# Router on the raw residual, its weights stationary in four column groups, in a hybrid decoder layer with 32 experts

## The chip, the cores and the metric

The kernel runs on one core of a Trainium2 chip. The metric is device time in microseconds (us) of one execution; the number for the kernel before is the median of three runs. A profile is one further execution, taken by the hardware profiler; its own span stands beside the median below.

## The reference

One layer over 256 tokens of width 1024: a mixer (gated linear attention and dilated window attention), a cross-attention into 256 memory tokens, a mixture of experts, and a final RMSNorm. What matters here is the third part:

```python
f = rms_norm(h, norm3_g)                       # h * rsqrt(mean(h^2) + eps) * g
logits = f @ w_router + b_router               # 256 x 32
top_logit, top_e = lax.top_k(logits, 4)
gate = jax.nn.softmax(top_logit, axis=-1)
# every token goes to its 4 experts e, weighted by gate:
glu = x @ w_gate[e] + b_gate[e]
lin = x @ w_up[e] + b_up[e]
y = clamped_swiglu(glu, lin) @ w_down[e] + b_down[e]
h = h + sum(gate * y)
out = rms_norm(h, final_norm_g)
```

All of it is in 32-bit floats. The 32 experts have three 1024 x 1024 matrices each: 12 MB an expert, 384 MB in all.

## The kernel before, in words

Five engines run their own instruction lists and meet at semaphores. Tokens lie in two tiles (t = 0, 1) of 128 partitions; `h` (128 x 2 x 1024) is the residual. PSUM has eight banks, and a table written out by hand (`FILLS`) gives each product its bank in turn; `take(name)` waits until the bank of that name is filled, `emptied(name)` until it has been read, `fill(name)` until it may be written again.

**Weights of the experts.** The ring in SBUF holds 16 slots of 1 MB. SyncE issues the loads in order, one 1 MB unit each, twelve units an expert (`load`, L381: four pairs of w_gate and w_up, then four of w_down). The first units are issued while the mixer and the cross-attention still run, as slots come free; sixteen are all the ring holds. Unit 16 and later wait in `slot_left` for TensorE to finish with the slot (L388): `gu_used` after a quarter of an expert's gate and up products, `dn_used` after a quarter of the down product.

**From the cross-attention to the first expert.** The output projection makes four banks `xo{n}{t}` (half n of the width, tile t; L1291). VectorE adds each to `h` (L1121), ScalarE squares the sum (`squares`, L556). TensorE then puts `h` into the four accumulator banks by products with the identity (L1539). `normed(3, ...)` sums the squares (L869), asks for the root (L822), GpSimd raises to -1/2 (`root`, L454), VectorE scales `h` into `f` (L872), TensorE transposes `f` (L1303), ScalarE and VectorE multiply by the norm's gain into `fT` (L760, L1128). The router follows: a product with ones for the bias (L1545), then for each of eight chunks of the width and each tile the 128 x 128 chunk of `fT` as weights and 32 columns of `w_rt` as the moving side (L1550). VectorE copies the logits (L1135), takes the largest eight and their places (L1138, L1141), makes the one-hot mask (L1146, L1148), then the gates (L1150 to L1153). TensorE counts places with a triangular matrix (L1556 to L1560) and transposes the gates (L1564), which ScalarE copies into `gateT`. Meanwhile ScalarE and VectorE cut `f` into two f16 parts in the memory of `h` (`f16`; L518, L1132).

**The experts** run as a loop over eight groups of four, the function `body(n, k)` on every engine. VectorE builds the selection matrices `sel` (L1178) and the gated ones `selG` (L1185). TensorE gathers the tokens of the group in four products (`gather`, L1584) through banks 2 and 3, of which `gather(2)` and `gather(3)` come after the first quarter of the first expert; ScalarE and VectorE multiply by the gain into `xg` (L781, L1192). Per expert j: gate and up products (L1624, two 64-column groups side by side), copies `hs` by ScalarE and VectorE (L518, L1197), transposes (L1638), the activation (L1208 to L1218), the down product (L1652) and the scatter into the accumulators (L1594).

## Time and profile before

| what | us |
|---|---|
| median of three runs (lowest, highest) | 1304.59 (1302.69, 1306.29) |
| span of the profiled execution | 1304.8 |
| TensorE busy | 1166.9 (89%) |
| VectorE busy | 413.0 (32%) |
| ScalarE busy | 279.5 (21%) |
| q1, the queue of the weight loads: bytes, share of 16 engines' span | 455.11 MB, 86.9% |

The profiled execution is 0.2 us above the median and inside the spread of the runs. In the page's chain of work that ended last TensorE has 57% and DMA 30%. The page also cuts the span in 40 slices of 32.6 us, each with a digit for the busy share of an engine and with what the DMA engines moved. Busy shares are averages over stages with different limits, so the stages have to be read one at a time.

### The profile page before, as it was taken

The page shows a single profiled execution, that of the slowest core. Times are in us where ns is not written, and L with a number is a line of the kernel's source. Part 1 is how long each engine was busy: PE and PEld are TensorE (multiplying, and loading weights), DVE is VectorE, ACT ScalarE, POOL GpSimd, SP SyncE. Part 2 cuts the span into 40 slices and gives each one's busy share as a digit, 9 for nine tenths or more (in the row PEclk, how much of TensorE's full clock was granted, in tenths as well). Part 3 has the DMA queues.
Part 4 walks back from the last instruction along what each step waited for, and adds up shares of the span by engine and source line. Part 5 has one row for each costly group of instructions (what it writes and reads, how often), then busy time and mean ns, then how long its engine had stood idle before and what let it go on. Part 6 is the DMA issues. An engine that isn't in the chain of part 4 may idle for free.

```text
span 1304.8 us, 16913 instructions
## 1 busy us (share of the span) xinstructions
PE 1166.9 (89%) x6669; PEld 596.7 (46%) x6669; DVE 413.0 (32%) x816; ACT 279.5 (21%) x475; POOL 20.2 (2%) x43
## 2 busy tenths in 40 slices
PE   6999999999899999898889988988988899889886
PEld 5888988987533333333323323322333233233322
DVE  5688454566411321121222112111212221121112
ACT  5655454455310020011002001100110020011001
POOL 3000000000000000000000000000000000000000
PEclk9999999999899999999999999999999999999997
DMA  8666443696299999999999999999999999999992
GB/s 277 194 194 191 146 128 105 220 366 266 85 371 423 421 422 421 422 422 422 422 422 422 422 422 421 422 422 422 422 423 421 422 422 422 422 422 422 422 422 105
DMA packets 103983, 458.00 MB, mean 351 GB/s; under 512 B 7324, under 2 KB 50392, under 8 KB 54792
## 3 DMA queue, kind: packets, MB, share of 16 engines
q1 hardware_dynamic: 103008, 455.11, 86.9%
q0 software_dynamic: 848, 2.32, 0.6%
q8 instruction: 28, 0.46, 0.1%
q14 instruction: 11, 0.09, 0.0%
q10 hardware_dynamic: 88, 0.02, 0.0%
HBM read 456.37 MB, written 1.05 MB: 351 GB/s over the span
## 4 chain that ended last, share of the span: by engine, by line
PE 57%; DMA 30%; DVE 6%; SPq 3%; issue 2%; ACT 2%; DVEq 0%; POOL 0%; POOLq 0%; ACTq 0%
DMA ring<-in_w_up 29%; PE bank L1624 19%; PE bank L1652 10%; PE bank L1268 7%; PE bank L1291 5%; PE bank L1341 5%; SPq L381 3%; PE bank L1584 2%; PE bank L1403 1%; DVE ring L843 1%; PE bank L1594 1%; PE bank L1638 1%; ACT ring L541 1%; DMA ring<-in_w_in 1%; DVE reg_g L1214 1%
## 5 line engine op out<-in xcount | busy, mean ns | idle before, releaser
L1624 PE MATMUL bank<-ring,reg_a 128*64 128x512 f32 x2048 | 457.9, 595 | 62.1 <-DMA ring<-in_w_up 60.1
L1624 PEld LDWEIGHTS bank<-ring,reg_a 128*64 128x64 f32 x2048 | 152.5, 137 | 355.3 <-issue 352.8
L1652 PE MATMUL bank<-ring,reg_g 128*64 128x512 f32 x1024 | 237.0, 617 | 20.9 <-DVE reg_g L1218 20.9
L1197 DVE COPY reg_t<-bank 128x512 f32<-128x512 f32 x32 | 22.1, 691 | 610.7 <-PE bank L1624 610.7
L518 ACT ACTIVATE reg_t<-bank 128x512 f32<-128x512 f32 x64 | 38.2, 597 | 678.3 <-PE bank L1624 473.7
L1652 PEld LDWEIGHTS bank<-ring,reg_g 128*64 128x64 f32 x1024 | 73.0, 141 | 178.5 <-issue 135.8
L843 DVE SCALAR_TENSOR_TENSOR ring<-ring 128x2048 f16<-128x2048 f32 x36 | 82.2, 2289 | 46.7 <-ACT ring L541 46.6
L541 ACT ACTIVATE ring<-ring 128x2048 f16<-128x2048 f32 x36 | 68.3, 1908 | 17.2 <-PE bank L1341 6.8
L1594 PE MATMUL bank<-reg_t,reg_g 64*128 64x512 f32 x256 | 63.6, 615 | 5.6 <-ACT reg_t L518 5.6
L1268 PE MATMUL bank<-reg_a,ring 128*128 128x256 f16 x576 | 65.4, 276 | 2.8 <-DVE reg_a L851 2.8
L1341 PE MATMUL bank<-reg_a,ring 128*128 128x256 f16 x576 | 63.2, 273 | 0.0
L1268 PEld LDWEIGHTS bank<-reg_a,ring 128*128 128x128 f16 x576 | 56.6, 99 | 11.7 <-DVE ring L843 3.2
L1341 PEld LDWEIGHTS bank<-reg_a,ring 128*128 128x128 f16 x576 | 56.3, 98 | 6.8 <-issue 0.3
L1291 PE MATMUL bank<-ring,reg_a 128*128 128x256 f16 x480 | 53.4, 273 | 0.0
L1638 PE MATMUL bank<-ident,reg_t 128*128 128x128 f32 x256 | 34.1, 276 | 21.1 <-DVE reg_t L1197 21.1
L1291 PEld LDWEIGHTS bank<-ring,reg_a 128*128 128x128 f16 x480 | 46.6, 98 | 5.9 <-issue 0.2
L792 ACT ACTIVATE reg_g<-reg_g 128x256 f32<-128x256 f32 x64 | 26.7, 417 | 100.8 <-DVE reg_g L1209 100.7
L1638 PEld LDWEIGHTS bank<-ident,reg_t 128*128 128x128 f32 x256 | 27.4, 140 | 42.0 <-ACT reg_t L518 41.5
L1192 DVE TENSOR_TENSOR reg_a<-bank,g 128x512 f32<-128x512 f32 x16 | 11.1, 692 | 91.7 <-PE bank L1584 91.7
L1594 PEld LDWEIGHTS bank<-reg_t,reg_g 64*128 64x128 f32 x256 | 22.0, 186 | 31.7 <-issue 19.1
L1208 DVE TENSOR_TENSOR reg_g<-bank,bT 128x256 f32<-128x256 f32 x64 | 26.8, 419 | 22.0 <-PE bank L1638 22.0
L1584 PE MATMUL bank<-reg_t,h 128*128 128x256 f16 x256 | 32.2, 282 | 0.9 <-ACT reg_o L518 0.9
(248 smaller groups left out, 811.7 us busy)
## 6 DMA issues: line engine op xcount, KB each, us to landing
ring<-in_w_gate SPq DMA_DIRECT2D x128, 1024.0 KB, 26.5
ring<-in_w_up SPq DMA_DIRECT2D x128, 1024.0 KB, 26.9
ring<-in_w_down SPq DMA_DIRECT2D x128, 1024.0 KB, 26.9
ring<-in_w_in SPq DMA_DIRECT2D x24, 1024.0 KB, 5.6
ring<-in_w_branch_gate SPq DMA_DIRECT2D x8, 1024.0 KB, 5.2
ring<-in_w_xkv SPq DMA_DIRECT2D x4, 1024.0 KB, 4.9
ring<-in_w_mix_out SPq DMA_DIRECT2D x4, 1024.0 KB, 5.2
ring<-in_w_branch_gla SPq DMA_DIRECT2D x2, 1024.0 KB, 4.9
```

The costliest lines, as they stand in the source:

```text
L381: sp.dma_start(slot[s], src.rearrange("e p n -> p (e n)")).then_inc(late_ld[s], 16)
L518: return act.activation(dst, src, ACT.Copy)
L541: ins = act.activation(cut[u % EARLY][:, 0, :], raw[u % EARLY], ACT.Copy, scale=WS)
L843: ins = dve.scalar_tensor_tensor(cut[u % EARLY][:, 1, :], raw[u % EARLY], WS, cut[u % EARLY][:, 0, :], ALU.mult, ALU.subtract)
L1268: ins = mm(b[:, i * T:(i + 1) * T], w[:, pw, c, o:o + P], rhs[:, px, c, :], start=(c == 0 and k == 0), stop=(c == nk - 1 and k == 2))
L1291: ins = mm(b[:, i * n:(i + 1) * n], lhs[:, px, c, t * P:(t + 1) * P], w[:, pw, c, 0:n], start=(c == 0 and k == 0), stop=(c == nk - 1 and k ...
L1341: ins = mm(b[:, i * T:(i + 1) * T], w[:, pw, i, c, :], aT[:, px, c, :], start=(c == 0 and k == 0), stop=(c == C - 1 and k == 2))
L1584: ins = mm(pt[2 + q % 2][:, i * T:(i + 1) * T], f16[:, part, t, 2 * q + i, :], sel[:, t, :], start=(t == 0 and part == 0), stop=(t == TT - ...
L1594: mm(acc[t][nh][:], selT[rows_h, j, t, :], y[rows_h, :], start=False, stop=False)
L1624: ins = mm(pt[nh][col:col + 64, :], xe[c], w[:, i, nh * 512:(nh + 1) * 512], start=(c == 0), stop=(c == C - 1))
L1638: ins = pe.transpose(pt[i][:, c * P:(c + 1) * P], hs[:, 4 * i + c, :], ident[:])
L1652: ins = mm(pt[2][64 * nh:64 * nh + 64, :], actT[:, c, :], w[:, i, nh * 512:(nh + 1) * 512], start=(c == 0), stop=(c == C - 1))
```

## The change

- The router works on `h` before the norm's scale. TensorE transposes `h` itself (`residual_T`): the first quarter ahead of the last output bank `xo11`, the others behind it. ScalarE and VectorE multiply by the gain (`routed_T`) as before; the first quarter is multiplied ahead of ScalarE's last squares, the second ahead of VectorE's sum of squares, the fourth while GpSimd makes the root.
- The router's product has `w_rt` (128 x 32) as weights and `fT` (256 columns) as the moving side; chunk c goes to the 32 output partitions of column group c mod 4. VectorE copies the result (`rtp`), and a product with `fold` (four stacked 32 x 32 identities, made once at the start) adds the groups and turns the logits token by token. The norm's scale and the bias, now broadcast to all partitions, are applied to the logits.
- The f16 parts are cut from `h` with the norm's scale and lie in the region of the former `f`. VectorE cuts the low parts in two halves (`f_lows`): one after the mask, one in the first group.
- The accumulator's products with the identity move: tile 0's behind the router, tile 1's behind the counts.
- The first group of experts is peeled off the loop. The low parts' second half, the reciprocal and the gates are computed there by VectorE behind `sel`; the gates' transposes run between the first two experts, and ScalarE copies `gateT` there.
- Channels are in chunks of 128 in place of strides of 8: w_gate, w_up, w_down, w_router and norm3_g are laid out anew on the host, the biases' transposes read contiguously, and the copies `hs` are contiguous. TensorE waits for ScalarE's half of `hs` before its first four transposes and for VectorE's before the other four.

```diff
-FILLS += [f"f_T{i}" for i in range(4)] + ["rt", "pos", "all", "gT"]
+FILLS += [f"f_T{i}" for i in range(4)] + ["rt", "rl", "pos", "all"]
@@ expert_groups
-            with eng.Fori(0, GROUPS) as n:
-                body(n, n)
+            body(0, 0, True)
+            with eng.Fori(1, GROUPS) as n:
+                body(n, n, False)
@@ scalar
+            def routed_T(q):
                 b = take(act, f"f_T{q}")
                 for i in range(2):
                     c = 2 * q + i
                     ins = act.activation(fT[:, c, :], b[:, i * T:(i + 1) * T], ACT.Copy, scale=g3[:, c:c + 1])
                 ins.then_inc(free_bank(f"f_T{q}"), 1)
+            for n in range(2):
+                for t in range(TT):
+                    emptied(act, f"xo{n}{t}")
+                    squares(3, h, xn, t, n, 512)
+                    if (n, t) == (1, 0):
+                        routed_T(0)
+            routed_T(2)
+            act.wait_ge(root_done, 6)
             for t in range(TT):
-                copy(f16[:, 0, t], f[:, t]).then_inc(f_high, 1)
+                act.activation(f16[:, 0, t], h[:, t, :].rearrange("p (c n) -> p c n", c=C), ACT.Copy,
+                               scale=st[:, 6 + t:7 + t]).then_inc(f_high, 1)
@@ vector
-            normed(3, 2, lambda t: h[:, t, :].rearrange("p (q c) -> p c q", c=C), lambda t: f[:, t], 6)
+            routed_T(1)
+            squared[0] += TT * 2
+            dve.wait_ge(norm_ss, squared[0])
+            link(dve.reduce_sum(st[:, 6:8], ssq[:, 3, :, 0:2], AX))
+            dve.tensor_scalar(st[:, 6:8], st[:, 6:8], 1.0 / D, EPS, ALU.mult, ALU.add).then_inc(root_asked, 1)
+            roots[0] += 1
+            routed_T(3)
+            b = take(dve, "rt")
+            dve.tensor_copy(rtp, b[:, 0:T]).then_inc(free_bank("rt"), 1)
+            dve.wait_ge(root_done, roots[0])
+            b = take(dve, "rl")
             for t in range(TT):
+                ins = dve.scalar_tensor_tensor(logit[:, t, :], b[:, t * E:(t + 1) * E], st[:, 6 + t:7 + t], b_rt[:],
+                                               ALU.mult, ALU.add)
...
             dve.reduce_sum(mask, hot.rearrange("p (t k) e -> p t e k", t=TT), AX).then_inc(gate_ready, 1)
-            dve.wait_ge(top_exp, 2)
-            link(dve.reciprocal(st[:, 54:56], st[:, 54:56]))
...
+            f_lows(0)
             b = take(dve, "pos")
...
+            def gates_and_lows():
+                f_lows(1)
+                dve.wait_ge(top_exp, 2)
+                link(dve.reciprocal(st[:, 54:56], st[:, 54:56]))
...
@@ vector, body, behind sel
+                if first:
+                    gates_and_lows()
+                    dve.wait_ge(gate_ready, 2)
@@ tensor
             for n in range(2):
                 w = weights(f"xo{n}")
                 for t in range(TT):
+                    if (n, t) == (1, 1):
+                        residual_T(0)
                     token_major(f"xo{n}{t}", w, oxT, 4, (t,), 512, ...)
+            for q in range(1, 4):
+                residual_T(q)
+            pe.wait_ge(ld_route, 48)
+            b = fill("rt")
+            for c in range(C):
+                if c % 2 == 0:
+                    emptied(pe, f"f_T{c // 2}")
+                j = c % 4
+                ins = mm(b[32 * j:32 * j + 32, 0:T], w_rt[:, c, :], fT[:, c, :], start=(c < 4), stop=(c >= 4))
+            filled(ins, "rt")
+            emptied(pe, "rt")
+            b = fill("rl")
+            for t in range(TT):
+                ins = mm(b[:, t * E:(t + 1) * E], rtp[:, t * P:(t + 1) * P], fold[:], start=True, stop=True)
+            filled(ins, "rl")
...
+            residual(0)
             pe.wait_ge(gate_ready, 1)
...
+            residual(1)
@@ tensor, body
                     if q >= 2:
                         pe.wait_ge((xg_act, xg_dve)[q - 2], 2 * k + 1)
+                        if first:
+                            pe.wait_ge(f_low, 2 * TT)
...
+                    if first and j == 1:
+                        gates_T()
...
-                    pe.wait_ge(hs_act, k * EG + (j + 1))
-                    pe.wait_ge(hs_dve, k * EG + (j + 1))
                     for i in range(2):
+                        pe.wait_ge((hs_act, hs_dve)[i], k * EG + (j + 1))
                         for c in range(4):
                             ins = pe.transpose(pt[i][:, c * P:(c + 1) * P], hs[:, 4 * i + c, :], ident[:])
@@ kernel (host)
+    for name in ("w_gate", "w_up", "w_down"):
+        w = np.asarray(inputs[name])[0]
+        inputs[name] = w.reshape(E, C, P, D).transpose(0, 2, 1, 3).reshape(E, P, C * D)
```

## Rows read from the trace of the kernel before

**Rows 1.** The page's slices: what the DMA engines moved, 40 slices of 32.6 us.

```profile
GB/s 277 194 194 191 146 128 105 220 366 266 85 371 423 421 422 421 422 422 422 422 422 422 422 422 421 422 422 422 422 423 421 422 422 422 422 422 422 422 422 105
```

**Rows 2.** Stages: busy us (instructions) of PE, PEld, DVE, ACT, POOL; PEclk; DMA share; GB/s.

```profile
340.00:360.00 20.00, 16.14 (x93) 11.40 (x94) 11.17 (x29) 6.90 (x15) 0.00 (x0) 0.74 0.09 32
360.00:365.00 5.00, 5.00 (x33) 2.62 (x34) 0.69 (x1) 0.84 (x2) 0.00 (x0) 1.00 0.81 297
...
1100.00:1200.00 100.00, 86.74 (x410) 32.32 (x410) 21.48 (x53) 11.32 (x20) 0.00 (x0) 0.98 1.01 422
```

**Rows 3.** The chain that ended last, near its end: start, us, what.

```profile
1244.61 26.92 DMA ring<-in_w_up
...
1271.66 3.67 PE bank L1624 x16
```

**Rows 4.** SyncE's queue in order of time: start, us, the loads it issued.

```profile
335.97 0.33 SPq L381 DMA_DIRECT2D ring<-in_w_up  x1
360.04 0.33 SPq L381 DMA_DIRECT2D ring<-in_w_gate  x1
...
365.48 0.33 SPq L381 DMA_DIRECT2D ring<-in_w_gate  x1
```

**Rows 5.** The chain that ended last, 335.9 to 362 us: start, us, what.

```profile
335.98 0.70 DVE h L1121
...
337.90 0.72 POOL st L454
...
338.65 2.21 DVE reg_m L872 x2
...
340.91 1.75 PE bank L1303 x14
...
343.02 4.34 PE bank L1550 x32
...
347.63 0.30 DVE reg_l L1138 x2
...
349.15 0.60 DVE route L1148
...
352.55 0.43 issue
352.99 3.43 PE bank L1584 x16
356.42 3.58 PE bank L1624 x16
```

**Rows 6.** Groups by line and form: busy us, mean ns of one | idle before.

```profile
L1128 DVE TENSOR_TENSOR reg_a<-bank,g 128x512 f32<-128x512 f32 x2 | 1.4, 692 | 1.1 <-PE bank L1303 1.0
L1132 DVE TENSOR_TENSOR h<-reg_m,h 128x1024 f16<-128x1024 f32 x2 | 2.4, 1222 | 0.7 <-ACT h L518 0.7
L1185 DVE TENSOR_TENSOR reg_g<-reg_t,route 128x512 f32<-128x512 f16 x2 | 1.3, 686 | 0.1
L1135 DVE COPY reg_l<-bank 128x64 f32<-128x64 f32 x1 | 0.2, 223 | 0.9 <-PE bank L1550 0.9
```

**Rows 7.** TensorE in order of time: start, us, operation, count, idle before it.

```profile
311.48 3.62 PE L1493 MATMUL bank<-reg_l 128*128 128x256 f32 x16
...
335.78 3.60 PE L1539 MATMUL bank<-h,ident 128*128 128x512 f32 x8
...
359.94 1.92 PE L1584 MATMUL bank<-reg_t,h 128*128 128x256 f16 x16
...
361.79 10.52 PE L1624 MATMUL bank<-ring,reg_a 128*64 128x512 f32 x48
```

**Rows 8.** VectorE in order of time, columns as in Rows 7.

```profile
350.50 0.58 DVE L1153 TENSOR_REDUCE route<-reg_g 128x64 f32<-128x256 f32 x1
...
351.69 0.76 DVE L1178 TENSOR_TENSOR reg_t<-route,iota_s 128x256 f16<-128x256 f32 x2
```

**Rows 9.** Granted clock of TensorE (PEclk) in one stretch; columns as in Rows 2.

```profile
346.00:356.00 10.00, 6.69 (x32) 5.21 (x32) 6.31 (x24) 3.36 (x9) 0.00 (x0) 0.50 0.00 0
```

More of the change, by code:

```diff
@@ L208, in _program @@
         hs = region(reg_t, 0, C, P)
+        rtp = region(reg_t, 0, T)
         y = region(reg_t, 1024, 512)
@@ L750, in _ @@
             x_out_T(1)
-            for n in range(2):
-                for t in range(TT):
-                    emptied(act, f"xo{n}{t}")
-                    squares(3, h, xn, t, n, 512)
             act.wait_ge(ld_route, 48)
-            for q in (0, 2):
+            def routed_T(q):
                 b = take(act, f"f_T{q}")
@@ L771, in _, with body @@
             copy(totals, b[:, 0:E]).then_inc(free_bank("all"), 1)
-            b = take(act, "gT")
-            copy(gateT[0:E, :], b[0:E, 0:T]).then_inc(free_bank("gT"), 1)
-            def body(n, k):
+            def body(n, k, first):
                 for q in (0, 2):
@@ L1122, in _, with routed_T @@
                         .then_inc(free_bank(f"xo{n}{t}"), 1)
-            normed(3, 2, lambda t: h[:, t, :].rearrange("p (q c) -> p c q", c=C), lambda t: f[:, t], 6)
             dve.wait_ge(ld_route, 48)
-            for q in (1, 3):
+            def routed_T(q):
                 b = take(dve, f"f_T{q}")
@@ L1527, in _, with residual_T @@
             x_out(1)
+            def residual_T(q):
+                b = fill(f"f_T{q}")
+                for t in range(TT):
+                    emptied(pe, f"xo{q // 2}{t}")
+                    for i in range(2):
+                        c = 2 * q + i
+                        ins = pe.transpose(b[:, i * T + t * P:i * T + (t + 1) * P], h[:, t, c * P:(c + 1) * P], ident[:])
+                filled(ins, f"f_T{q}")
             for n in range(2):
@@ L1535, in _, with residual @@
                 pe.wait_ge(free[b], USES[b])
-            for n in range(2):
-                for t in range(TT):
-                    emptied(pe, f"xo{n}{t}")
+            def residual(t):
+                for n in range(2):
                     mm(acc[t][n][:], ident[:], h[:, t, n * 512:(n + 1) * 512], start=True, stop=False)
-            norm_transposes("f_T", lambda t, c: f[:, t, c, :], 8)
-            pe.wait_ge(ld_route, 48)
-            b = fill("rt")
-            mm(b[:, 0:TT * E], ones[0:1, :], mid(b_rt[:], TT), start=True, stop=False)
-            for c in range(C):
-                if c % 2 == 0:
-                    emptied(pe, f"f_T{c // 2}")
-                for t in range(TT):
-                    ins = mm(b[:, t * E:(t + 1) * E], fT[:, c, t * P:(t + 1) * P], w_rt[:, c, :], start=False,
-                             stop=(c == C - 1 and t == TT - 1))
-            filled(ins, "rt")
+            residual(0)
             pe.wait_ge(gate_ready, 1)
@@ L1560, in _, with gates_T @@
             filled(mm(b[:, 0:E], ones[:], mask[:, 1, :], start=False, stop=True), "all")
-            pe.wait_ge(gate_ready, 2)
-            b = fill("gT")
-            for t in range(TT):
-                ins = pe.transpose(b[0:E, t * P:(t + 1) * P], gate[:, t, :], ident[:])
-            filled(ins, "gT")
+            residual(1)
+            def gates_T():
+                pe.wait_ge(gate_ready, 2)
+                for t in range(TT):
+                    ins = pe.transpose(pt[3][0:E, t * P:(t + 1) * P], gate[:, t, :], ident[:])
+                ins.then_inc(gT_full, 1)
             for b in range(4):
@@ L1572, in _, with body @@
             per = 12 * EG
-            def body(n, k):
+            def body(n, k, first):
                 pe.wait_ge(sel_ready, k + 1)
@@ L1614, in body @@
                     v = 12 * j
+                    if first and j == 1:
+                        gates_T()
                     xe = [xg[:, c, j * SLOTS:(j + 1) * SLOTS] for c in range(C)]
@@ L1657, in body @@
                 scatter(EG - 1)
+                if first:
+                    pe.wait_ge(gT_done, 1)
             expert_groups(pe, body)
```

51 lines of the change are left out of this document (31 added, 20 removed).

## The prediction

> **What bounds the kernel now.** I read the slices first. From slice 12 to slice 38 (counted from 0) the DMA engines move 421 to 423 GB/s without a break, and just before, in slice 10, 85 GB/s [rows 1]. So 27 of 40 slices stream expert weights at one constant rate. A stage closer up gives the same: 422 GB/s at a DMA share of 1.01 from 1100 to 1200 us, while TensorE is busy 86.74 of the 100 us [rows 2]. The chain at the end says so too: the last gate and up product starts at 1271.66 us when a load of w_up has just landed, and only 33 us of work follow it [rows 3]. The expert stage is bound by bytes.
>
> The second thing to see is the hole before it. From 340 to 360 us the DMA share is 0.09 [rows 2]: all sixteen slots are full. SyncE issues unit 15 at 335.97 and the next one only at 360.04 [rows 4], when TensorE has finished the first quarter of the first expert. After that instant 368 units of 1 MB (1.049 million bytes) remain, at 422 GB/s 2.485 us each, 914 us. Nothing later in the stage makes up for a late start, and nothing takes back an early one. **The end follows the instant at which that first slot is released**, one us for one us. The work on the change is thus the chain from the last add into `h` (335.98) to the end of the first gate and up quarter (356.42 + 3.58 = 360.00), 24.0 us [rows 5].
>
> **The change along that chain.** I walk it with durations of before; the new clock time stands behind each step.
>
> 1. `residual_T(0)` goes ahead of the last output bank: four transposes. Fourteen took 1.75 us [rows 5], so four cost 0.5. The add starts at 336.45. This is the one new cost at the head.
> 2. Add, squares, sum and root request take as before 335.98 to 337.90: GpSimd's root starts at 338.4 and ends at 339.1. The other twelve transposes hide here, but for the half of them that wait for the add (337.2); the last ends at 338.1. GpSimd issues its two late loads (b_down, the final gain) half a us later too, and is still free by then.
> 3. Removed: the scaling of `h` into `f`, 2.21 us, the transposes behind it, 1.75, the bias product and the router's 32 short products, 4.34 [rows 5]. In their place: `routed_T(3)` on VectorE behind the root request, 0.69 [rows 6], to 339.1. ScalarE's `routed_T(2)` ends at 338.9, so the fourth quarter is the last. Then the last two of eight router products. One product of 256 columns is two instructions of 3.62/16 = 0.226 us [rows 7]. Two products side by side in their column groups are 0.45, one after the other 0.9. That groups of 64 columns run side by side is in the trace: 16 instructions of 512 columns in 3.58 us [rows 5], 0.22 each, against 3.60/8 = 0.45 for one over all columns [rows 7]. I take 0.45 and 0.1 for the semaphores: filled at 339.7 to 339.9. The first six are done by then.
> 4. Added: the copy `rtp` of 128 x 256. 128 x 64 took 0.22 and 128 x 512 took 0.69 [rows 6]; between them, 0.42. To 340.25. Then the fold, four instructions with full weights; L1550's went at 4.34/32 = 0.136 each [rows 5], so 0.6 with its start. Then two scalings of 128 x 32, at most 0.22 each [rows 6]: the first of the top-8 instructions starts at 341.35, against 347.63 [rows 5]. **6.3 us gained so far.**
> 5. From there to the mask is unchanged, 347.63 to 349.75 or 2.1 us [rows 5]: 343.5.
> 6. VectorE then has `f_lows(0)`, two instructions of 512 elements. An f16 low part of 1024 took 1.22 [rows 6]; half of it is 0.61, two are 1.25, to 344.75. Removed from this place: the gates' arithmetic, from 349.75 to 351.08, 1.3. Even. Placing and `sel` take what they took, 351.08 to 352.45 or 1.4 [rows 8]: ready at 346.15. The count products are hidden beside `f_lows(0)`.
> 7. TensorE's own queue: counts from 343.55, eight instructions at 0.136, to 344.6; then `residual(1)`, four instructions of 512 columns at 0.45 [rows 7], 1.8 us, to 346.4. So TensorE and VectorE arrive within 0.2 us of each other. `residual(0)` (341.0 to 342.8) hides beside the top-8. All eight of these instructions were hidden beside the norm before; if the clock is low they are not.
> 8. Removed: the gates' transposes, the copy to `gateT` and the 0.43 of issue between it and the first gather at 352.99 [rows 5]. Added in the first group: 0.3 us of transposes at the second expert. There TensorE is ahead of the loads, so this costs nothing; without that slack it would cost 0.3.
> 9. First gathers: 3.43 us [rows 5], at a granted clock of 0.50, that is 1.2 GHz [rows 9]. The same sixteen took 1.92 at the full 2.4 GHz [rows 7]. Starting at 346.45 with the full clock, they end at 348.4; the gain's multiply for the first quarter ends by about 348.5. The quarter of gate and up, 3.6 us, ends at **352.15 against 360.00: 7.85 us.**
>
> **What could hold the next slots.** The second pair of loads went out 5.4 us after the first [rows 4]. For that pair `gather(2)` waits for all low parts and `gather(3)` for VectorE's `xg`. Behind `sel` VectorE has `f_lows(1)` 1.25, gates 1.4 [rows 8], `selG` 1.35 [rows 6], `xg` 0.7: from 346.15 to 350.9, while TensorE asks at 352.15. 1.2 us of slack; queued behind these are only the activations of the first expert, ten us later. The DMA stage after the release is therefore a copy of the old one, shifted. Contiguous `hs` copies cost the same (one PSUM read per element), and the split wait gives at most 0.1 at the tail. The weights' new layout keeps 8 KB a partition at the same strides, so 422 GB/s stays. `fold` (0.2 us) and a broadcast bias are at the start, where VectorE waits for `x`: nothing.
>
> One rule to weigh. Step 3 leans on column groups, and the rows show two groups at twice the pace. The Trainium skill (TensorEngine Tiling (Array Packing), Theoretical Speedup and Key Properties) grants up to four times for 32 columns, but says that changing the tiling mode drains the engine. By the first half the eight products would be 0.9 us instead of 1.8, without effect, since the last pair waits for `routed_T(3)`; by the second, two changes would cost a drain each. No run yet shows four groups; at a change from the whole array to 64 columns the trace shows no gap: the gathers end at 361.86 and L1624 starts at 361.79 [rows 7].
>
> **Rivals.**
> - *The clock stays low.* Before, it was at 0.50 from 346 to 356 [rows 9], and what ran ahead of the fall was 4.34 us of 32-column products. After, TensorE from 338 to 345 has about 0.9 to 1.8 us of router, 1.8 of identity products, the fold and the counts, with holes between. If it falls there, the counts go from 1.1 to 1.9, `residual(1)` from 1.8 to 3.6, the gathers from 1.95 to 3.43: 4.1 us at most, leaving 3.75, or 1300.8. A fall for part of it costs 1.5 to 3: 5.6 left, about 1299. For it: nearly the same holes. Against it: dense 512- and 256-column products in place of the 32 short ones.
> - *Column groups one after the other.* The last pair costs 0.45 more and the six before it, 2.7 us from 338.1, end at 340.8: in all 1.8 late. 6.0 gained, 1298.5. The rows with two groups speak against it.
> - *The gain is not kept.* If the loads were starved after the early restart (from 360 to 365 us they moved 297 GB/s, not 422 [rows 2]) because slots are released late in the first group, the gain would go there: 1302 to 1304. Against: the steps between releases are the same as before.
> - *Slower.* VectorE's queue in the first group: `gather(2)` and `gather(3)` stand behind 4.8 us of new order, with 1.2 of slack. Each us beyond is paid in full; slower than before by over 0.3% needs 12.9 us beyond the plan there, say from the strided one-hot arithmetic of the gates taking ten times its 1.2 us. It would give 1309. The rows of exactly these instructions speak against it.
>
> **How the numbers follow.** The profiled span, 1304.8, is 0.2 above the median 1304.6. Likeliest is the full chain: 7.85, less 0.3 for some ten new semaphore handoffs at 0.03, so 7.5: 1304.6 - 7.5 = **1297.1**. Chances: 0.52 for this, 0.28 for the low clock, 0.08 for the groups in a row, 0.09 for no lasting gain, 0.03 for slower. The range takes in the first three and the spread of the runs (1.9 below to 1.7 above the median): 1295.2 to 1301.2. What can be told from no change is 0.3%, 3.9 us: faster 0.86, same 0.11, slower 0.03.
>
> **What the profile after would show.** First load behind the hole issued at about 352.5 instead of 360.04; top-8 at 341.4; `sel` ready at 346.15; PEclk above 0.9 from 340 to 356 if the likeliest case holds, two sixteens of L1584 of nearly 1.95 us each; 422 GB/s after. Wrong would be: a gather that waits for VectorE in the first group, eight router products taking over 2 us, DMA below 415 GB/s between 400 and 1200 us, or an end that moves less than the first load does.

## The result, and the profile after

The changed kernel takes 1294.45 us (median of 4 runs, 1292.22 to 1295.37) against 1304.32 for the kernel before in the same series (4 runs, 1302.69 to 1306.29): ratio 0.9923, 95% interval 0.991 to 0.9936. That is 9.9 us gained where 7.5 were forecast, and 0.75 us below the low end of the range. A second series, with 17 runs of the kernel before, gives 1294.75 against 1303.47, or 8.7. All series together, 47 runs of the one and nine of the other, have medians of 1304.09 and 1294.75: 9.3 us. One further execution of the kernel before, of 1556 us at a granted clock of 0.745, is left out of every comparison. The gain is real and larger than forecast; how much larger, the runs tell only to about a microsecond.

The profiled execution after spans 1293.0 us; its device time is 1294.88. Two later profiled executions of the kernel before have spans of 1304.7 and 1304.0 and device times of 1306.49 and 1305.79. So the span is 1.8 to 1.9 us shorter than the device time of the same execution. The 1304.8 of the profile before thus belongs, by this estimate, to an execution of about 1306.6 us, not to the median.

The slices after, beside [rows 1]: 120 GB/s in slice 10, 417 in slice 11 where 371 stood, the same 420 to 422 behind it.

```profile
GB/s 280 178 206 176 158 116 115 229 339 311 120 417 422 420 420 421 421 422 422 422 422 422 422 421 422 422 422 422 422 422 422 421 422 422 422 422 422 422 422 141
```

Stages after (columns as in [rows 2]). Between 340 and 352 the granted clock is 1.00 where [rows 9] had 0.50; the expert stage is the one of before to a digit.

```profile
340.00:352.00 12.00, 10.93 (x57) 5.77 (x57) 9.27 (x29) 2.72 (x8) 0.00 (x0) 1.00 0.20 64
352.00:357.00 5.00, 5.00 (x31) 2.37 (x31) 0.69 (x1) 0.84 (x2) 0.00 (x0) 1.00 0.89 336
...
1100.00:1200.00 100.00, 86.76 (x410) 32.21 (x408) 19.01 (x46) 8.33 (x17) 0.00 (x0) 0.98 1.01 422
```

SyncE's queue after, beside [rows 4]: the first load behind the hole goes out at 351.60 instead of 360.04, the next pair 5.45 us later (5.44 before).

```profile
336.14 0.33 SPq L384 DMA_DIRECT2D ring<-in_w_up  x1
351.60 0.33 SPq L384 DMA_DIRECT2D ring<-in_w_gate  x1
...
357.05 0.33 SPq L384 DMA_DIRECT2D ring<-in_w_gate  x1
```

The chain of waits after, between the last add and the release (start, us, what), beside [rows 5]:

```profile
336.14 0.70 DVE h L1134
...
336.89 0.88 PE bank L1574 x6
337.77 0.57 PE bank L1592 x8
...
338.37 0.92 PE bank L1592 x8
...
339.31 0.44 DVE reg_t L1161
...
339.79 0.65 PE bank L1597 x4
...
340.54 0.42 DVE reg_l L1165 x2
...
340.99 0.30 DVE reg_l L1170 x2
...
342.50 0.60 DVE route L1180
...
344.22 1.80 PE bank L1606 x4
346.02 0.89 PE bank L1644 x8
...
347.91 3.65 PE bank L1686 x16
```

The reader is to see what is no longer there: no scaling of the residual, no 32 short products, no transposes of the gates ahead of the first gather (L1644). From the fill of the first gate and up quarter to the last loads the chain is the old one. The end of the stream, beside [rows 3]:

```profile
1233.41 26.98 DMA ring<-in_w_up
...
1260.53 3.67 PE bank L1686 x16
```

**Where the 11.8 us between the two profiled spans come from.** I cut each execution at three instants that both kernels have: X, the start of the attention's output projection (325.05 before, 324.79 after), the issue of the first load behind the hole, and the start of the last gate and up product. All numbers in the table are differences of such instants, in us.

| profiled execution | to X | X to first load | first load to last gate/up | from there to the end | span |
|---|---|---|---|---|---|
| before (shown above) | 325.05 | 34.99 | 911.62 | 33.14 | 1304.8 |
| after | 324.79 | 26.81 | 908.93 | 32.47 | 1293.0 |
| difference | 0.26 | **8.18** | 2.69 | 0.67 | 11.8 |

The stretch that the change touches gives 8.18, near the 7.85 of the prediction. The other 3.6 us lie outside it. Most of the experiments go to the question what those are: a result of the change, or of the one execution that was profiled.

**Two small parts of them are the change's own**, and the rows show both. The first lies long before X. The sixteen transposes of the experts' biases used to read every eighth number of a row and now read it contiguously. TensorE in order of time, before and after:

```profile
83.70 1.94 PE L1354 MATMUL bank<-ident,ring 32*128 32x32 f32 x16
```

```profile
85.56 1.18 PE L1393 MATMUL bank<-ident,ring 32*128 32x32 f32 x16
```

The median weight load there fell from 202 to 137 ns. TensorE has no slack in this part (from 50 to 250 us it is busy throughout in both), and the time is kept: from the start of the mixer's first run of 192 product instructions (30.03 before, 31.89 after) to the first scores of the cross-attention (311.48 and 312.58) it is 281.45 us before and 280.69 after. Taken in every profile of this document, it is 281.44 to 281.46 in the four with the old front part and 280.67 to 280.70 in the ten with the new one: **0.77 us**. No run puts the old reading back alone; the row and the stretch around it, equal in all else, are the evidence. The column "to X" hides this, because the profiled execution after reached that run 1.86 us later, and the one before lost 1.4 us in the cross-attention, as shown below. The second part is the split wait for `hs`, worth **0.15 us** at the end; it is shown below, where the wait is put back. With the chain that makes 8.18 + 0.77 + 0.15 = 9.1 us.

### The profile page after: what moved, and what is told of

Read it like the earlier page. It is cut to its first block, busy times and chain, and to the rows that moved or that the text cites. A ratio compares the mean times of both kernels' runs of the same rounds, so it can differ in the third digit from the quotient of the medians.

```text
span 1293.0 us, 16762 instructions
## 1 busy us (share of the span) xinstructions
PE 1162.2 (90%) x6655; PEld 594.6 (46%) x6655; DVE 411.7 (32%) x819; ACT 260.5 (20%) x460; POOL 20.2 (2%) x43
## 4 chain that ended last, share of the span: by engine, by line
PE 60%; DMA 28%; DVE 6%; ACT 3%; issue 2%; SPq 2%; DVEq 0%; POOL 0%; POOLq 0%; ACTq 0%
DMA ring<-in_w_up 27%; PE bank L1686 22%; PE bank L1713 11%; PE bank L1307 7%; PE bank L1330 5%; PE bank L1380 5%; PE bank L1644 2%; SPq L384 2%; PE bank L1442 1%; DVE ring L854 1%; PE bank L1654 1%; ACT reg_t L521 1%; PE bank L1699 1%; ACT ring L544 1%; DMA ring<-in_w_in 1%
## 5 line engine op out<-in xcount | busy, mean ns | idle before, releaser
L1686 PEld LDWEIGHTS bank<-ring,reg_a 128*64 128x64 f32 x2048 | 154.6, 137 | 351.6 <-issue 349.3
L851 DVE SCALAR_TENSOR_TENSOR ring<-ring 128x1024 f16<-128x1024 f32 x24 | 28.3, 1222 | 8.9 <-ACT ring L542 8.6
```

The lines of the kernel that those rows point to most:

```text
L851: ins = dve.scalar_tensor_tensor(dst, src, WS, rotary_cut(u, 0, i)[0], ALU.mult, ALU.subtract)
L1686: ins = mm(pt[nh][col:col + 64, :], xe[c], w[:, i, nh * 512:(nh + 1) * 512], start=(c == 0), stop=(c == C - 1))
```

## The experiments

In each, the profile is read in the four stretches of the table; the time is the median, with the kernel before on the same chip and in the same series (1303.47 for the change once more, the delay in the release, the clock in the first expert and the two waits, 1304.82 for the four from the router without column groups to the moved identity products, 1304.34 for the last two).

**The change once more.** No edit.

> The changed kernel once more, timed beside the kernel before. Two theories stand. Path theory: the end follows the first released slot one for one and everything beyond the chain's gain (8.4 us in the first profile: first load behind the hole at 351.60 instead of 360.04) is spread between runs; then the medians differ by 8 to 9 us. Stream theory: 1 to 2 us more are won lastingly behind that release (the loads are not starved a second time, the tail is shorter); then the medians differ by 9.5 to 10.5 us, and in this profile too the time from the first load behind the hole to the last gate and up product is nearer to 908.9 us (changed kernel) than to 911.6 us (kernel before).

Measured: 1294.75 us (5 runs), ratio 0.9933 (0.992 to 0.9946). X to the first load 26.81, the stream 909.09, the end 32.47: the profile repeats to 0.2 us. So the gain in the chain is no accident of one execution.

**A delay put into the release alone.** Four products with the identity, each of 512 columns, ahead of the first gate and up product.

```diff
                 gather(1)
+                if first:
+                    for _ in range(4):
+                        mm(pt[0][:], ident[:], h[:, 0, 0:512], start=True, stop=True)
```

> The changed kernel with four products of the identity with 512 columns (3.6 us) put between the second gather and the first gate product of the first group; they write a bank that the gate product overwrites. Path theory: the first load behind the hole goes out 3.6 us later and the end moves by 3.6 us against the changed kernel. Rival (the expert stage absorbs it, since TensorE is 5 us an expert faster than the loads): the end moves by less than 1 us.

Measured: 1297.91 us, ratio 0.9959 (0.9946 to 0.9972), 3.16 more than the change in the same series. TensorE, then SyncE, of this kernel, in order of time:

```profile
346.91 3.60 PE L1675 MATMUL bank<-h,ident 128*128 128x512 f32 x8
```

```profile
354.13 0.33 SPq L384 DMA_DIRECT2D ring<-in_w_gate  x1
```

X to the first load is 30.03 instead of 26.81, 3.22 more. The end moved by 3.16. This is the claim on which the prediction stands: the end follows the release one for one, so 8.2 us of earlier release are worth about 8.2 us. That the two numbers agree to 0.06 is in part luck. In four of the variants below (one group, norm first, gates early, the better version) the shift of the release and that of the median differ by 0.5 to 1.6 us.

**Does a low clock in the first expert cost stream time?** In the profile before, TensorE's first down product (L1652) took 8.78 us, partly at the low clock, and the loads fell to 359 GB/s at the same time; after, it took 7.09 and the loads kept 415. To see whether this is a cause, the kernel before gets four more products in each group's gap ahead of that product.

```diff
                         pe.wait_ge(selT_dve, k + 1)
+                        for _ in range(4):
+                            mm(pt[3][:, 0:256], ident[:], w_rt[:].rearrange("p c e -> p (c e)"), start=True, stop=True)
```

> The kernel before with four products of the identity with 256 columns (1.8 us) in every group's gap before the first expert's down product, into a bank that is free then; only the clock should change. Stream theory: the down product of the first expert runs 7.1 instead of 8.8 us, its slots come free earlier, the loads keep 420 GB/s in the five us from 380 to 385 us instead of 359, and the end is 0.7 to 1.2 us earlier than the kernel before. Path theory: no change (within 0.3 us).

Measured: 1303.29 us (12 runs), ratio 1.0 (0.999 to 1.0009). In its profile the down product took 7.09, the loads dipped nowhere, and the stream took 909.22, as after. And the median moved by no more than 0.2 us. So this was not worth 2 us in the usual execution. The two profiles that follow say why: in both the down product took 8.78 us at the low clock again, and yet their streams took 909.86 and 909.16. The slow down product belongs to the kernel before; the long stream was that of one execution. The low clock of the routing stage was untouched; this kernel's windows (columns as in [rows 2]):

```profile
346.00:348.60 2.60, 2.32 (x21) 2.21 (x20) 2.28 (x3) 0.60 (x1) 0.00 (x0) 1.00 0.00 0
348.60:358.80 10.20, 7.18 (x30) 4.64 (x32) 6.35 (x23) 3.37 (x9) 0.00 (x0) 0.50 0.00 0
```

**Two more profiles of the kernel before.** No edit.

> The kernel before once more, for its profile. In its first profile the time from the first load behind the hole to the last gate and up product is 911.6 us, and 359 GB/s moved from 380 to 385 us; in six profiles of the changed kernel and its variants it is 908.9 to 909.8. If the dip belongs to the kernel before, this profile shows it again (911 or more); if it is chance, 909 to 910.

> The kernel before a third time, for its profile: as the run before_a. Besides, how far the start of the output projection and the first slot's release (34.99 us apart in the first profile, 26.8 in three profiles of the changed kernel and one variant) move between executions of one program.

Measured: streams of 909.86 and 909.16 us, X to the first load 35.13 and 34.98, spans 1304.7 and 1304.0. The 2.69 of the stream in the table above falls to 0.2 to 0.9. The 359 GB/s don't return: at the same distance from the release the first of them moved 400. But their spans are as long as before, because the time is lost elsewhere: X lies at 328.28 and 326.81. TensorE in order of time, the cross-attention's products with the values in the first of these two, and the same in the kernel after:

```profile
322.61 3.40 PE L1512 MATMUL bank<-reg_g,reg_l 128*128 128x256 f32 x8
```

```profile
320.75 1.89 PE L1551 MATMUL bank<-reg_g,reg_l 128*128 128x256 f32 x8
```

All four profiled executions of before's front part show these eight instructions at the low clock (2.85 to 3.53 us), of ten with the change's front part two. They stand ahead of the output projection and so of the part that the change reworks (of its edits only `fold`, the broadcast bias and the biases' transposes come earlier, all before 90 us). What makes the clock fall there, and whether it is tied to the kernel, stays open. The slow products cost 1.4 to 1.7 us: from the first scores to X it is 13.57 to 13.89 us with them and 12.20 or 12.21 without. If every execution before had them and every one after did not, the medians would differ by over 10 us (9.1 and these), and they don't.

**Both waits in front of the eight transposes of `hs`**, as before the change.

```diff
+                    pe.wait_ge(hs_act, k * EG + (j + 1))
+                    pe.wait_ge(hs_dve, k * EG + (j + 1))
                     for i in range(2):
-                        pe.wait_ge((hs_act, hs_dve)[i], k * EG + (j + 1))
```

> The changed kernel with the wait before the activation's transposes put back: all eight wait for ScalarE's and VectorE's half of hs. The last expert's chain behind the last loads gets 0.15 to 0.2 us longer; the experts before it have slack. Both theories: 0.1 to 0.3 us slower than the changed kernel; 0.5 us or more would mean that the split wait carries a part of the surplus.

Measured: 1294.8 us, 0.05 from the change in the same series (0.9935, 0.9923 to 0.9948); X to the first load 26.81. The median doesn't show the split wait; the end of the trace does, beside the change. TensorE in order of time, the last expert's transposes, here and after:

```profile
1259.22 3.65 PE L1686 MATMUL bank<-ring,reg_a 128*64 128x512 f32 x16 [1.30 <-DMA ring<-in_w_up]
1263.75 1.07 PE L1700 MATMUL bank<-ident,reg_t 128*128 128x128 f32 x8 [0.88 <-DVE reg_t L1236]
```

```profile
1264.87 1.10 PE L1699 MATMUL bank<-ident,reg_t 128*128 128x128 f32 x8 [0.69 <-ACT reg_t L521]
```

The transposes start 4.53 us behind the last gate and up product here and 4.34 after. From that product to the last scatter it is 15.46 or 15.47 us in this profile and the four with the old kernel, and 15.30 to 15.32 in the nine with the split wait: 0.15 us, as expected.

**Router without column groups.** All eight products go to the same 32 output partitions; the fold becomes a plain transpose.

```diff
-                j = c % 4
-                ins = mm(b[32 * j:32 * j + 32, 0:T], w_rt[:, c, :], fT[:, c, :], start=(c < 4), stop=(c >= 4))
+                ins = mm(b[0:32, 0:T], w_rt[:, c, :], fT[:, c, :], start=(c == 0), stop=(c == C - 1))
```

> The changed kernel with all eight router products in one column group, one after the other; the fold is then a plain transposing product over 32 partitions. In the profile of the changed kernel eight instructions before the last wait took 0.57 us and the last eight 0.92 us. If the column groups carry a part of the gain: the sixteen instructions take 3.6 us of product time instead of 1.5, the logits come 1.5 to 2 us later and the end moves by as much. If the waits for the gained transposes carry it, the end moves by less than 0.5 us.

Measured: 1297.33 us (6 runs), ratio 0.9945 (0.9927 to 0.9962). TensorE in order of time, here and after:

```profile
337.42 3.64 PE L1591 MATMUL bank<-reg_a,w_rt 128*32 128x256 f32 x16
```

```profile
337.70 1.56 PE L1592 MATMUL bank<-reg_a,w_rt 128*32 128x256 f32 x16
```

In one group the sixteen instructions take 3.64 us, 0.23 each. In four groups they take 1.56, and that includes a wait for the last quarter of the operand; the chain shows the first eight of them in 0.57. X to the first load is 2.05 later. The Trainium skill (TensorEngine Tiling (Array Packing), Theoretical Speedup) allows up to four times for 32 columns; the 0.57 us for eight are 3.2 times the pace of 0.228 each, so here the page holds. The drain at a change of mode that it names under Key Properties doesn't show as a gap: transposes over the whole array end at 337.77 in the chain, and the router is under way at once.

**The norm's scale put back onto `h` ahead of the transposes.** The transposes read the scaled copy, so that all four quarters and the multiplies by the gain move behind the norm, and the logits are no longer scaled.

```diff
+            dve.wait_ge(root_done, roots[0])
+            for t in range(TT):
+                dve.tensor_scalar(fn[:, t], h[:, t, :], st[:, 6 + t:7 + t], None, ALU.mult).then_inc(norm_xn, 1)
+            routed_T(1)
             routed_T(3)
...
-h[:, t, c * P:(c + 1) * P], ident[:])
+fn[:, t, c * P:(c + 1) * P], ident[:])
```

> The changed kernel with the norm's scale back in front of the router: VectorE scales h into another region behind the root, TensorE transposes that, and the logits get no scale. Everything else stays. Prediction's step 3: the scaling of two tiles (1.4 to 2.2 us), the transposes (1.8) and the multiplies come back onto the chain, 3.5 to 4.5 us in all, and the end moves by as much. Rival (TensorE's clock made most of the chain's gain): less than 2 us.

Measured: 1298.74 us (9 runs), ratio 0.9961 (0.9949 to 0.9974). X to the first load 31.95, 5.14 later than the change. The raw residual is the largest single part of the 8.2, though not 5.14 of it: some 1.8 us are slow transposes that the kernel before did not have (its fourteen took 1.75 us [rows 5], the sixteen here 3.78). What ended last, TensorE in order of time and the window around it:

```profile
339.46 3.78 PE L1577 MATMUL bank<-ident,reg_g 128*128 128x128 f32 x16 [3.68 <-DVE reg_g L1160]
```

```profile
339.60:343.10 3.50, 3.43 (x16) 2.88 (x15) 1.06 (x2) 1.48 (x4) 0.00 (x0) 0.51 0.66 227
343.50:348.00 4.50, 3.57 (x24) 1.41 (x16) 2.80 (x14) 2.45 (x6) 0.00 (x0) 1.00 0.00 0
```

TensorE stood idle for 3.68 us, and just as it started again the granted clock fell: it was 1.00 up to 339.50, then 0.51, so that the transposes took 3.78 us, and only 3.5 us later it was 1.00 again. The hole costs twice: its own length, and the slow transposes behind it.

**The gates' arithmetic back ahead of `sel`.**

```diff
             f_lows(0)
+            dve.wait_ge(top_exp, 2)
+            link(dve.reciprocal(st[:, 54:56], st[:, 54:56]))
+            ...
+            dve.reduce_sum(gate, hot_g.rearrange("p (t k) e -> p t e k", t=TT), AX).then_inc(gate_ready, 1)
             b = take(dve, "pos")
```

> The changed kernel with the reciprocal and the gates' arithmetic (1.45 us on VectorE) back in front of the places. The selection is ready 1.45 us later; since TensorE arrives 0.45 us after the selection in the changed kernel, the first gathers start 1.0 us later and the end moves by 1.0 us. Rival (TensorE's queue with the identity products is what sets the start): 0.

Measured: 1294.35 us (6 runs), ratio 0.992 (0.9905 to 0.9934). The expected 1.0 us doesn't show in the time: the release is 1.22 us later from X, TensorE waits 1.06 us for `sel`, and the median is no worse than that of the change. The row (TensorE, in order of time), and why the time hides it:

```profile
346.73 1.91 PE L1644 MATMUL bank<-reg_t,reg_m 128*128 128x256 f16 x16 [1.06 <-DVE reg_t L1214]
```

```profile
1281.89 1.99 PE bank L1727 x4
```

The second row is from the chain at the end of this profile: the last four output products in it took 1.99 us, and 3.48 in the profile after. This execution's end took 30.41 us instead of 32.47. A granted clock that falls or holds at the last handful of instructions moves the end by as much as this edit does. So one microsecond is below what medians of six runs can assign; the release shows it, the time does not.

**The identity products of tile 1 moved into the first group's gap**, ahead of `hs`' transposes, where TensorE waits anyway.

```diff
-            residual(1)
...
                         scatter_matrices()
+                    if first and j == 0:
+                        residual(1)
```

> The changed kernel with the second tile's products of the identity (1.8 us on TensorE) moved from behind the counts into the gap before the first expert's transposes. The selection is ready at 345.58 and TensorE starts to gather at 345.86 to 346.02 in the changed kernel: the gathers start 0.3 to 0.45 us earlier, and the end is earlier by as much. Rival: the products then delay the first expert's transposes and its slots, so the loads starve: 0 to 1 us slower.

Measured: 1297.32 us (6 runs), ratio 0.9943 (0.9927 to 0.9959): about 3 us slower than the best of the same series, though it takes 1.8 us out of TensorE's way. TensorE in order of time, then three windows:

```profile
344.34 3.38 PE L1643 MATMUL bank<-reg_t,reg_m 128*128 128x256 f16 x16 [1.50 <-DVE reg_t L1214]
```

```profile
344.00:347.40 3.40, 3.06 (x15) 2.21 (x16) 3.26 (x8) 0.84 (x2) 0.00 (x0) 0.50 0.00 0
```

```profile
371.35:376.35 5.00, 5.00 (x25) 1.76 (x22) 0.05 (x1) 0.00 (x0) 0.00 (x0) 1.00 0.95 341
376.35:381.35 5.00, 5.00 (x26) 1.73 (x26) 0.00 (x0) 0.85 (x2) 0.00 (x0) 1.00 0.93 377
```

Two costs. VectorE's `sel` ended last anyway, so the gathers began only 0.15 us earlier; and in the 1.50 us for which TensorE now had nothing to do, the clock fell to 0.50, and the sixteen gathers took 3.38 us instead of 1.91. And 1.8 us of work in the gap delayed the following slots: the loads dipped to 341 and 377 GB/s, and the stream took 911.12. The result doesn't need the identity products at their place in the change, and yet they save time there: they are what TensorE is busy with while VectorE makes `sel`. This is the rival "the clock stays low" made to happen in part, by removing work. From X the release is 1.12 us later.

**A delay in the gap alone**, two identity products (1.8 us) right behind the first gate and up products, so that only the later slots move.

```diff
+                    if first and j == 0:
+                        for _ in range(2):
+                            mm(pt[2][:], ident[:], h[:, 0, 0:512], start=True, stop=True)
                     if j == 0:
                         scatter_matrices()
```

> The changed kernel with two products of the identity with 512 columns (1.8 us) put behind the last gate and up product of the very first expert, ahead of its transposes; the clock stays high, the first load behind the hole is not touched, but the slots of the first down product come free 1.8 us later. If a second dip of the loads costs lastingly: 340 to 380 GB/s some 20 us behind the restart, the stretch to the last gate and up product 911 instead of 909.1 us, and the end 1.2 to 2.3 us later. If TensorE's lead absorbs it: less than 0.4 us.

Measured: 1295.23 us (6 runs), ratio 0.9926 (0.9911 to 0.9941). The release is untouched (26.81), but the expectation that the clock stays high failed: the first down product started 1.8 us later and then took 8.70 us, not 7.09, in part at the low clock. So this is not a delay of 1.8 us alone. Two windows of 5 us, 20 us behind the release:

```profile
370.95:375.95 5.00, 5.00 (x24) 1.68 (x22) 0.27 (x1) 0.00 (x0) 0.00 (x0) 0.85 0.82 288
375.95:380.95 5.00, 5.00 (x26) 1.61 (x24) 0.00 (x0) 0.85 (x2) 0.00 (x0) 1.00 0.97 360
```

In this profile the stream took 911.83, 2.9 more than after; the bytes missing from the two windows against 422 GB/s are 5 x (0.318 + 0.147) = 2.3 us. By the median the price is 0.5 to 0.8 us against the change in its two series, neither of them taken beside this kernel. A dip behind delayed slots is what the two experiments with a late gap share (in the one before, the down product ran at full speed, 7.09 us); what it costs in the usual execution is not settled.

**A better version.** VectorE cuts tile 0's low half ahead of the places and tile 1's behind `sel`; half of `residual(1)` stays behind the counts, the other half goes behind the gates' transposes.

```diff
-            f_lows(0)
+            f_lows(0, (0,))
...
-                f_lows(1)
+                f_lows(0, (1,))
                 f_lows(1)
...
-            residual(1)
+            residual(1, (0,))
...
                         gates_T()
+                        residual(1, (1,))
```

> The changed kernel with VectorE's low parts for the first gathers split: tile 0 ahead of the places, where VectorE waits for the counts anyway, tile 1 behind the selection; and with only one half of the second tile's identity products behind the counts, the other between the first two experts. The selection is ready 0.7 us earlier and TensorE is free 0.9 us earlier. Gathers 0.6 to 0.8 us earlier, if the clock stays high the end is 0.6 to 0.8 us earlier than the changed kernel; if the clock falls, as it did without any identity product there, the gathers take 3.4 instead of 1.9 us and it is 0.5 to 1 us slower.

Measured: 1293.55 us (1293.35 to 1294.12, 5 runs), ratio 0.9915 (0.9899 to 0.9932), the lowest of all kernels here; its five runs lie within 0.8 us. TensorE in order of time:

```profile
342.48 1.10 PE L1607 MATMUL bank<-h,ident 128*128 128x512 f32 x2
343.64 2.17 PE L1646 MATMUL bank<-reg_t,reg_m 128*128 128x256 f16 x16
```

The gathers start 0.64 us earlier from X (20.43 instead of 21.07) and take 0.26 more, since the second half of their operand comes from VectorE as they go; the release is 0.38 earlier. The granted clock stayed at 1.00 with half of the identity products in that place. The kernel's difference to the change, 0.9 to 1.2 us by medians of different series, is more than its 0.38 of release, and within what the ends scatter.

## Why the prediction was right in its mechanism and counted too little

The chain and its release were forecast rightly. Two steps failed: the chain's gain was cut from 7.85 to 7.5 where it measured 8.18, and everything outside the chain was put at nothing where the rows show 0.92 us.

**Step 1** put the add at +0.5. The four transposes took 0.44 in the chain. Right.

**Steps 2 to 4** forecast the first top-8 instruction at 341.35; it started at 340.99. The last eight router instructions took 0.92 in the chain, waits included, and the first eight 0.57. The copy `rtp` was 0.44 against 0.42, the fold 0.65 against 0.6, the two scalings 0.42 against at most 0.44.

**Step 5**, the mask: 343.08 (342.50 + 0.58) against 343.5; 2.1 us from the top-8, as said. **Step 6**, `sel`: 345.58 against 346.15. The low parts took 1.41 where I had 1.25 from half of an instruction of 1024; placing and `sel` behind them took 1.25 (344.33 to 345.58) where I had 1.4. VectorE in order of time:

```profile
343.01 1.41 DVE L1150 SCALAR_TENSOR_TENSOR reg_m<-h,st,reg_m 128x512 f16<-128x512 f32 x2
...
344.82 0.42 DVE L1214 TENSOR_TENSOR reg_t<-route,iota_s 128x256 f16<-128x256 f32 x1
...
345.16 0.42 DVE L1214 TENSOR_TENSOR reg_t<-route,iota_s 128x256 f16<-128x256 f32 x1
...
349.52 0.69 DVE L1231 TENSOR_TENSOR reg_a<-bank,g 128x512 f32<-128x512 f32 x1
```

**Step 7**: TensorE and VectorE should arrive within 0.2 us of each other; TensorE was free at 345.86 to 346.0 and ended last, 0.3 to 0.4 behind `sel`. **Step 9**: the gathers at full clock took 1.91 (1.92 said), and the release came at 351.60 against 352.15. These instants are 0.4 to 0.6 early, but 0.26 of that is the earlier X of this execution; counted from X they are only 0.1 to 0.3 early. The likeliest case, full clock throughout, held in the profile after and in its replicate. That identity products hold the clock was an argument in the prediction; their removal bears it out, in one profile and in the median of its six runs.

**What could hold the next slots**: I gave VectorE 1.2 us of slack in the first group, with `xg` ready at 350.9. It was ready at 350.21, and TensorE asked for it behind the quarter that ended near 351.6: 1.4 us of slack, and no row of a wait. The stage behind the release is a copy of the old one: pairs of loads 5.45 us apart, 300 GB/s in the first 5 us (303 before).

So the chain was worth 8.18 (8.17 to 8.32 between any two profiles of the two kernels) where the prediction had 7.85. The larger error lies in what was done with that number, in the paragraph on how the numbers follow, and in what was left out of it:

- **"Less 0.3 for some ten new semaphore handoffs"** had nothing to take off. Steps 3 and 4 already have time for semaphores and a start in them, and even so the instants came early. With the 7.85 rounded down as well, this and the chain's own 0.33 are 0.7 us.
- **Nothing outside the chain.** Of the start the prediction counts `fold` and the broadcast bias, at nothing. The biases' transposes, which the change reads contiguously, stand in no step, and they are worth 0.77 us. The split wait, "at most 0.1", is worth 0.15. Together 0.92 us.
- **The base.** 1304.6 was the median of three runs. The three larger series of the kernel before gave 1303.47, 1304.82 and 1304.34, the pooled 47 runs 1304.09. A base known to 1 us was taken as known to 0.
- **"The spread of the runs (1.9 below to 1.7 above the median)"** was the only room below the forecast. It stands for one execution's scatter and left none for a gain outside the walked chain. By the medians there is one: 9.3 pooled less 8.2 is 1.1 us (0.5 in the one series, 1.7 in the other), and 0.92 of it are the two parts above. What remains, 0.2 pooled, -0.4 in the one series and 0.8 in the other, is scatter as far as these runs tell. The profiles show where such scatter sits: the cross-attention's products at the low clock (3.40 against 1.89 us) ahead of the chain, and 30.4 to 33.3 us for the end by whether the last products were slow. All four profiles of the kernel before or its variant show the former and only two of ten of the change's; that the change is the cause isn't shown.
- **Span against median.** I set the span of 1304.8 equal to the median of 1304.6. The span is 1.9 short of its own execution's time, so the profiled executions before were 1 to 2 us above the median of the timed ones. Whoever subtracts two spans here gets 11.8, too much by 2 or 3.

Put together for the series of the result: 1297.1 less 1294.45 is 2.65 us, of which 0.28 are the base, 0.68 chain, handoffs and rounding, 0.92 the two small parts outside the chain, and 0.77 stay unexplained. With the measured terms the sum would have been 1304.6 less 9.1, or 1295.5. The steps that failed are the sum's term for the chain, cut to 7.5 where 8.18 was measured, and the zero for all else where 0.92 was measured; the range, with only the scatter of three runs below the forecast, left no room for either. The mechanism stood.

**The rivals.** The low clock did not come in the routing stage, and its place and price are shown by moving `residual(1)`: the gathers 1.5 us longer. Column groups one after the other: eight products in a single group cost 2.05 us against the 1.8 that the prediction gave for this rival, and four groups don't run like that. The gain not kept: excluded by the delay of 3.2 us that came back as 3.16. The other variants agree with that less closely (release later by 2.05, 5.14 and 1.22 us, median by 2.6, 4.0 and -0.4), which is the accuracy of such medians. In the prediction, the price set for "slower" did not add up either: ten times 1.2 us are 10.8 more, not the 12.9 needed. Slower by VectorE's queue: it had 1.4 us in hand.

## What to carry to other kernels

Where a stream of fixed rate follows a hole, find the one instant that ends the hole, walk the chain to it with rows, and test the claim with a pure delay at that instant. Before work on TensorE that seems to be in the way is moved to idle time elsewhere, look at what the engine would do instead: work that covers a wait can be cheaper than the low clock behind an idle stretch. Price every edit, also one made for another purpose: here the same stretch, taken between the same two products in all profiles, repeats to 0.03 us and shows 0.77 us that the medians could not. And give a forecast more room than the scatter of a few runs: the base moves by a microsecond between series, and stretches that nobody touched differ between executions by as much.

## What the runs showed of the hardware that was not expected

- TensorE's clock fell within a stretch in which it was busy. In the kernel before it was busy without a break from 343.00 to 346.00, with the router's 32-column products, and in the last half microsecond of that the granted clock fell; from 346 on it was 0.50, that is 1.2 GHz. In the variant with more products in the gaps it was busy for 2.32 of the 2.60 us up to 348.60, and from there the clock was 0.50 for 10.2 us. With the change it was 1.00, or 2.4 GHz, over the same stage. The windows of the kernel before (columns as in [rows 2]):

```profile
343.00:345.50 2.50, 2.50 (x24) 2.50 (x23) 1.81 (x3) 1.99 (x3) 0.00 (x0) 1.00 0.03 7
345.50:346.00 0.50, 0.50 (x6) 0.50 (x5) 0.50 (x1) 0.00 (x0) 0.00 (x0) 0.88 0.00 0
```

- The clock came back within the slow work itself: 0.51 for 3.5 us over the sixteen transposes behind an idle 3.68 us, then 1.00; and 0.50 for 3.4 us over the gathers behind an idle 1.50 us, then 1.00 for the gate and up products.
- Transposes in f32 that read every eighth number of a row are slower than contiguous ones: weight loads of 202 against 137 ns, sixteen transposes of 32 by 128 in 1.94 against 1.18 us.
- Four column groups of 32 run side by side in f32 at 3.2 times the pace of one, with no gap where the whole array's work ends.
- A late restart of loads costs its own length and no more (3.22 for 3.16), but work in the gap of the first expert is followed by a second dip 20 us later (341 and 377 GB/s; 288 and 360 where the down product was slow as well), and in those profiles the stream was 2.2 and 2.9 us longer.
- The same program's executions differ by where the clock falls: eight products in the cross-attention took 1.89 or 3.40 us, the last four 1.99 or 3.48. For changes near 1 us the release instant in the profile is the better measure.
